# Three of eight token blocks by rows instead of two, with a shorter candidate list and dense sums held in PSUM

## The chip, the cores and the metric

The kernel runs on one core of a Trainium2 chip. The metric is the device time of one execution in microseconds. An execution is one launch from the inputs in HBM to the output in HBM.

## What is computed

A decoder layer: projections, retention and sliding-window attention, a first norm that gives h, and then the PEER feed-forward layer with which this case deals. For each of 1024 tokens and 8 heads, it finds the best 16 of 16384 experts by product keys and sums their outputs:

```
s1, i1 = lax.top_k(s[:, :, 0], K)          # K = 16 of 128 keys, two sides
s2, i2 = lax.top_k(s[:, :, 1], K)
cand = (s1[..., :, None] + s2[..., None, :]).reshape(T, H, K * K)
top_s, pos = lax.top_k(cand, K)            # 16 of 256 pairs
idx = take_along_axis(cand_idx, pos)       # 128 experts per token
g = softmax(top_s)
u = take(u_tab, ib); a = gelu(einsum('cd,ced->ce', xb, u)) * gb
y = einsum('ce,ced->cd', a, take(v_tab, ib))
```

All is float32; u_tab and v_tab have 16384 rows of 1024. The result is layer_norm(ALPHA * h + y).

## The kernel before

The program has five stages, each written engine by engine with its own order and semaphores. `project`, `attend` and `score` (queries, key scores, and the search for token blocks 0 and 1) come first. The last two stages hold the change.

The 1024 tokens are 8 blocks of 128. A block is worked in one of two ways. **Dense** blocks (6 of them) are multiplied with all 16384 experts on TensorE; a one-hot product makes a gate for every pair of token and expert, zero where the expert was not picked. **By rows** (the first GB = UB = 2 blocks), each token's 128 picked rows are gathered: one indirect DMA of GpSimd brings one row of 1024 for each of 128 tokens (0.5 MB), and VectorE makes a dot product or a weighted addition of it. Numbers of float32 go through TensorE in two parts, hi and lo, with three products each.

`experts_in` (z = U h) has 128 tiles of 128 experts in 8 turns of 16 tiles; a tile has two slots, 32 to a turn. Per tile TensorE does 24 products of 512 columns into z_first and 24 of 256 into z_rest, ACT and GpSimd split the tile (L795, L799), ACT reads z and sends it to HBM. Beside this, at slots fixed by tables:
- VectorE's `top_piece` searches one later block per turn in turns 0 to 5: 16 `side` searches in 128 scores, 8 `pairs` searches in 256 sums (L741, then L728 to L732), and 4 `names` (L756 to L764), which turn places into expert numbers for two heads.
- Gate steps, 32 per dense block, in turns FIRST = 2 to 7: one-hot on VectorE (L1273), scaling on ACT, product on TensorE, copy on ACT.
- Row products: GpSimd's gathers (L1215), VectorE's dot products (L1285), PER_TURN of them per turn, in RING = 3 buffers, EARLY = 2 ahead. `gather` waits until the product that used its buffer is done. GpSimd's tile splits stand in the same queue.

`experts_out` (y = V a) has 32 rounds of 4 tiles. Each round, for each dense block: ACT takes the gelu of z, VectorE multiplies by the gate (`product`, L1560), ACT and VectorE split into a_hi and a_lo (L1470, L1564), and TensorE does 2 x 12 products of 512 columns (L1443 to L1445) into two of eight PSUM banks used in turn; VectorE adds both to y in SBUF (`add`, L1572). V's tiles are split by ACT and VectorE (L1475, L1577). Rows of v (GpSimd L1508, VectorE `add_row` L1555) are spread over rounds 1 to 30, in four buffers, three ahead. In round r VectorE works through the blocks in steps: product(r), add(r - 1), split of v, lo of the block before, rows. y starts as ALPHA * h, loaded whole (L1591 scales it).

The buffers of `experts_out` that are filled ahead lie in one piece of memory, `room`, which earlier stages use for their own tiles; the trace calls all of them `room`.

## Time and profile before

| | us |
|---|---|
| three runs | 3078.61, 3078.38, 3083.45 (median 3078.61) |
| the profiled execution | 3082.5, its span 3080.7 |
| granted TensorE clock, mean | 0.985 |
| busy: TensorE 97%, VectorE 76%, ACT 39%, GpSimd 34% | 2980.4, 2327.8, 1204.8, 1053.0 |
| `experts_in` | 741.8 to 2005.8 |
| `experts_out` | 2005.8 to 3080.7 |
| moved by DMA | 693 MB, mean 225 GB/s |

The span is cut at the first product of a turn or of a round. A busy share is an average over stages with different limits, so the stretches are read one by one. Products on TensorE overlap, so their durations add up to more than the span; the price of one is the distance between starts.

### The profile page before, as it was taken

Reading aid. Unit: us, or ns where it says so; the run is one execution under the profiler, and the core shown is the slowest. Engines: PE = TensorE matmul, PEld = TensorE weight load, DVE = VectorE, ACT = ScalarE, POOL = GpSimd, SP = SyncE. Lnnn points to the kernel's source line nnn. Section 1 sums busy time; section 2 is a strip of 40 time slices with the busy share of each in tenths; the row PEclk is TensorE's granted clock in tenths of the full one; section 3 lists DMA queues with packets and bytes.
Section 4 is the critical chain, followed back from the end, with each engine's and each line's share of the span. In section 5 each row is a group of like instructions: output and inputs, shape, how many; then the busy total and the mean of one; then the engine's idle time right before and its main releaser. Section 6 shows DMA issues by size and latency. Waiting matters only on the chain. (4 is left out here: it accounts for less than half of the span.)

```text
span 3080.7 us, 42384 instructions
## 1 busy us (share of the span) xinstructions
PE 2980.4 (97%) x15866; PEld 2565.9 (83%) x15866; DVE 2327.8 (76%) x4289; ACT 1204.8 (39%) x2245; POOL 1053.0 (34%) x750
## 2 busy tenths in 40 slices
PE   7997998999999999999999999979999999999998
PEld 6887886888888899989898999868888888888887
DVE  4214775567988888888887556569998998999898
ACT  2112332222222566656566657533333333333331
POOL 3222221001455443443434454424433333333331
PEclk9997998999999999999999999989999999999999
DMA  4223222222677666666666888789988898888881
GB/s 169 84 89 123 104 97 83 72 79 69 236 247 255 228 225 234 223 246 241 240 231 250 288 299 301 290 297 317 321 299 302 283 313 292 295 307 296 298 306 74
DMA packets 291846, 693.46 MB, mean 225 GB/s; under 512 B 20304, under 2 KB 134352, under 8 KB 288464
## 3 DMA queue, kind: packets, MB, share of 16 engines
q1 hardware_dynamic: 189776, 315.61, 30.7%
q0 software_dynamic: 73728, 268.47, 24.4%
q10 hardware_dynamic: 28160, 106.96, 9.0%
q8 instruction: 113, 1.85, 0.2%
q14 instruction: 69, 0.57, 0.1%
HBM read 564.08 MB, written 126.88 MB: 224 GB/s over the span
## 5 line engine op out<-in xcount | busy, mean ns | idle before, releaser
L1443 PE MATMUL y_ps<-v_hi,a_hi 128*128 128x512 f32 x1536 | 600.1, 391 | 20.4 <-DVE y L1572 11.5
L1444 PE MATMUL y_ps<-v_lo,a_hi 128*128 128x512 f32 x1536 | 599.6, 390 | 0.0
L1445 PE MATMUL y_ps<-v_hi,a_lo 128*128 128x512 f32 x1536 | 599.4, 390 | 0.0
L799 POOL TENSOR_TENSOR u_lo<-u_raw,u_hi 128x1024 fp32r<-128x1024 f32 x128 | 314.6, 2458 | 725.0 <-ACT u_hi L795 724.0
L1104 PE MATMUL z_first<-hT_hi,u_hi 128*128 128x512 f32 x1024 | 409.9, 400 | 9.5 <-PEq L825 5.1
L1508 POOL DMA_INDIRECT v_rows<-in_v,room x192 | 259.7, 1353 | 463.1 <-DVE y L1555 439.2
L1106 PE MATMUL z_first<-hT_hi,u_lo 128*128 128x512 f32 x1024 | 401.3, 392 | 0.0
L1105 PE MATMUL z_first<-hT_lo,u_hi 128*128 128x512 f32 x1024 | 400.7, 391 | 0.0
L1443 PEld LDWEIGHTS y_ps<-v_hi,a_hi 128*128 128x128 f32 x1536 | 289.6, 189 | 81.6 <-issue 11.9
L1445 PEld LDWEIGHTS y_ps<-v_hi,a_lo 128*128 128x128 f32 x1536 | 289.6, 189 | 60.4
L1444 PEld LDWEIGHTS y_ps<-v_lo,a_hi 128*128 128x128 f32 x1536 | 289.6, 189 | 60.3
L1273 DVE TENSOR_TENSOR hot<-near,iT 128x1024 f32<-128x1024 f32 x192 | 234.1, 1222 | 124.2 <-PE g_ps L1114 122.2
L1572 DVE TENSOR_TENSOR y<-y_ps,y 128x512 f32<-128x512 f32 x384 | 255.2, 685 | 80.9 <-PE y_ps L1445 77.6
L1104 PE MATMUL z_rest<-hT_hi,u_hi 128*128 128x256 f32 x1024 | 297.0, 290 | 0.0
L1105 PE MATMUL z_rest<-hT_lo,u_hi 128*128 128x256 f32 x1024 | 289.7, 283 | 0.0
L1106 PE MATMUL z_rest<-hT_hi,u_lo 128*128 128x256 f32 x1024 | 289.6, 283 | 0.0
L1146 ACT ACTIVATE hot_g<-hot,gT 128x128 f32<-128x128 f32 x768 | 244.4, 390 | 77.7 <-DVE hot L1273 50.0
L1285 DVE CUSTOM_DVE_ANT_0 u_rows<-u_rows,h_ps 128x1024 f32<-128x1024 f32 x170 | 207.3, 1219 | 73.7 <-DMA u_rows<-in_u,room 62.0
L1555 DVE SCALAR_TENSOR_TENSOR y<-v_rows,a_rows,y 128x1024 f32<-128x1024 f32 x192 | 242.5, 1278 | 1.7 <-DMA v_rows<-in_v,room 1.7
L1475 ACT ACTIVATE v_hi<-room 128x1024 fp32r<-128x1024 f32 x128 | 135.4, 1058 | 271.7 <-DMA room<-in_v 267.9
L1104 PEld LDWEIGHTS z_first<-hT_hi,u_hi 128*128 128x128 f32 x1024 | 193.7, 189 | 46.4 <-issue 5.2
L1106 PEld LDWEIGHTS z_first<-hT_hi,u_lo 128*128 128x128 f32 x1024 | 193.3, 189 | 42.5
(195 smaller groups left out, 5829.4 us busy)
## 6 DMA issues: line engine op xcount, KB each, us to landing
u_raw<-in_uT SPq DMA_DIRECT2D x128, 512.0 KB
room<-in_v SPq DMA_DIRECT2D x128, 512.0 KB
z<-z_sb ACTq DMA_DIRECT2D x128, 384.0 KB
gates<-g_sb ACTq DMA_DIRECT2D x24, 2048.0 KB
room<-z SPq DMA_DIRECT2D x16, 1536.0 KB
z_in<-z SPq DMA_DIRECT2D x16, 1536.0 KB
g_in<-gates SPq DMA_DIRECT2D x16, 1536.0 KB
room<-gates SPq DMA_DIRECT2D x15, 1536.0 KB
```

The lines of the kernel that those rows point to most:

```text
L799: self.nc.gpsimd.tensor_tensor(self.u_lo[e][:], self.u_raw[e][:], self.u_hi[e][:].bitcast(F32), ALU.subtract).then_inc(self.u_lo_in[e], 1)
L1104: nc.tensor.matmul(o, u_hi[e][:, k], hT_hi[:, k, cols], start=(k == 0), stop=False)
L1105: nc.tensor.matmul(o, u_hi[e][:, k], hT_lo[:, k, cols], start=False, stop=False)
L1106: last = nc.tensor.matmul(o, u_lo[e][:, k], hT_hi[:, k, cols], start=False, stop=(k == KT - 1))
L1146: last = nc.scalar.activation(hot1_g[g][:, t], hot[g][:, 0, t], ACT.Copy, scale=gT[:, t0 + t:t0 + t + 1])
L1273: nc.vector.tensor_tensor(hot[g][:], bc(bc(iota_ps, 1, 4), 1, 2), bc(iT[:, :, t0:t0 + 4], 3, NK), ALU.is_equal).then_inc(hot_in[g], 1)
L1443: nc.tensor.matmul(o, ah, v_hi[p][:, i, c], start=(i == 0), stop=False)
L1444: nc.tensor.matmul(o, ah, v_lo[p][:, i, c], start=False, stop=False)
L1445: last = nc.tensor.matmul(o, al, v_hi[p][:, i, c], start=False, stop=(i == GROUP - 1))
L1508: nc.gpsimd.indirect_dma_start(out=rows_in[i % RING][:], out_offset=None, in_=d["v"].rearrange("a b c -> (a b) c"), in_offset=bass.Indirec ...
L1555: nc.vector.scalar_tensor_tensor(y[:, b], rows_in[i % RING][:], a_rows[:, b, slot:slot + 1], y[:, b], ALU.mult, ALU.add).then_inc(added[b], 1)
L1572: nc.vector.tensor_tensor(y[:, GB + s, c], y_ps[n % 8][:], y[:, GB + s, c], ALU.add).then_inc(y_read, 1)
```

## The change

Three blocks go by rows instead of two, five are dense. In `experts_in` the second half of a tile keeps 256 columns and the first shrinks to 384; there are six row buffers, three of them in `room` (two lie where the first tiles of v will be), and a new table of row products by turn, which ends in the middle of turn 7. Gate steps begin in turn 3. `pairs` searches 80 candidates instead of 256: a pair (a, b) of sorted lists can only be among the best 16 if (a + 1)(b + 1) is at most 16, and four rectangles hold all of these. `decode` turns a place among the 80 into a row and a column, for four heads at once, and `names` then runs twice in a row.

In `experts_out` two of the five dense blocks (HELD) stay in two PSUM banks each for all rounds and are added to y once, at the end. The other three share four banks; they are taken in alternating direction, so that the last of one round is the first of the next and goes on in its banks: two blocks are added per round. The load of h is cut into four, in another order, and ALPHA is applied in a block's first addition. RING and EARLY of this stage stay 4 and 3.

```diff
@@ constants
-GB = 2
+GB = 3
-UB = 2
+UB = 3
@@ class TopK
+    KEPT = [(0, 2, 16), (2, 2, 8), (4, 4, 4), (8, 8, 2)]
...
-        link(nc.vector.tensor_tensor(self.cand[:], bc(self.top[:, 0], 2, TOPK), bc(self.top[:, 1], 1, TOPK), ALU.add))
-        self.top16(link, self.cand[:].rearrange("p a b -> p (a b)"), self.cand_left[:],
-                   self.best[:, b % 2, h], self.pos[:, b % 2, h])
+        at = 0
+        for first, n, wide in self.KEPT:
+            part = self.cand[:, at:at + n * wide].rearrange("p (a c) -> p a c", c=wide)
+            last = nc.vector.tensor_tensor(part, bc(self.top[:, 0, first:first + n], 2, wide),
+                                           bc(self.top[:, 1, 0:wide], 1, n), ALU.add)
+            at += n * wide
+        link(last)
+        self.top16(link, self.cand[:], self.cand_left[:], self.best[:, b % 2, h], self.pos[:, b % 2, h])
...
+    def decode(self, link, b, half):
+
+        nc = self.nc
+        pos = self.pos[:, b % 2, half * PH // 2:(half + 1) * PH // 2]
+        row, col = self.ab[:, 0], self.ab[:, 1]
+        link(nc.vector.tensor_scalar(self.step, pos, 4, None, ALU.logical_shift_right))
+        link(nc.vector.tensor_scalar(self.step, self.step, 1, None, ALU.max))
+        nc.vector.tensor_scalar(self.past, self.step, 16, -16, ALU.mult, ALU.add)
+        link(nc.vector.tensor_scalar(self.step, self.step, -1, 5, ALU.mult, ALU.add))
+        link(nc.vector.tensor_tensor(col, pos, self.past, ALU.subtract))
+        link(nc.vector.tensor_tensor(row, col, self.step, ALU.logical_shift_right))
+        link(nc.vector.tensor_tensor(self.past, row, self.step, ALU.logical_shift_left))
+        link(nc.vector.tensor_tensor(col, col, self.past, ALU.subtract))
...
-        nc.vector.tensor_scalar(self.ab[:, 0], pos, 4, None, ALU.logical_shift_right)
-        link(nc.vector.tensor_scalar(self.ab[:, 1], pos, 15, None, ALU.bitwise_and))
@@ score
-                    if h % 2:
-                        tk.names(link, b, h // 2)
+                    if h % 4 == 3:
+                        tk.decode(link, b, h // 4)
+                        for two in range(2):
+                            tk.names(link, b, h // 4 * 2 + two)
@@ experts_in
-    RING, EARLY = 3, 2
+    RING, EARLY = 6, 5
-    PER_TURN = [24, 34, 27, 27, 27, 27, 45, 45]
+    PER_TURN = [50, 62, 62, 40, 40, 40, 60, 30]
...
+        rows_in = ahead.rows + ahead.v_raw
+        rows_in = rows_in + [sb(f"u_rows{i}", [P, D]) for i in range(RING - len(rows_in))]
...
+            first, end = 6 if s == 0 else 0, SLOTS // 2 if s == TB - 1 else SLOTS
...
+                        sp.wait_ge(h_taken, UB)
...
+                        sp.wait_ge(row_used, UB * PH * TOPK)
                         for e in range(2):
                             sp.dma_start(ahead.v_raw[e][:], d["v"][e]).then_inc(ahead.v_here[e], 16)
...
-                    elif n == 6:
-                        tk.names(link, b, q)
-                    elif n == 7 and q == Q - 1:
-                        v.wait_ge(exps, b + 1)
-                        tk.gates(link, b)
+                    elif n == 6 and q % 2:
+                        tk.decode(link, b, q // 2)
+                        tk.names(link, b, q - 1)
+                    elif n == 7 and q % 2:
+                        tk.names(link, b, q)
+                        if q == Q - 1:
+                            v.wait_ge(exps, b + 1)
+                            tk.gates(link, b)
@@ experts_out
+        HELD = (0, DB - 1)
+        CYCLED = list(range(1, DB - 1))
+        LAST = len(CYCLED) - 1
+
+        def order(r):
+
+            if r == 0:
+                return [HELD[0], *CYCLED[:2], HELD[1], *CYCLED[2:]]
+            return [HELD[0], *(CYCLED[::-1] if r % 2 else CYCLED), HELD[1]]
+
+        def run(r, s):
+
+            return LAST * r + (LAST - CYCLED.index(s) if r % 2 else CYCLED.index(s))
+
+        def banks(r, s):
+
+            first = 2 * HELD.index(s) if s in HELD else 4 + 2 * (run(r, s) % 2)
+            return y_ps[first:first + 2]
+
+        def opens(r, s):
+
+            return r == 0 or (s not in HELD and run(r, s) > LAST * r)
+
+        def closes(r, s):
+
+            return r == NG - 1 or (s not in HELD and run(r, s) < LAST * (r + 1))
+
+        def made(r):
+
+            return order(max(r - 1, 0))
...
                 load_v(0, first=2)
+                load_h(slice(GB + 1, TB - 1), cycled_here)
                 load_z(1)
-                sp.dma_start(y[:], d["h"].rearrange("n p c -> p n c")).then_inc(h_here, 16)
+                load_h(slice(0, GB), rows_here)
                 load_v(1)
+                load_h(slice(GB, GB + 1), held_here)
+                load_h(slice(TB - 1, TB), held_here)
...
-                        nc.tensor.matmul(o, ah, v_hi[p][:, i, c], start=(i == 0), stop=False)
+                        nc.tensor.matmul(o, ah, v_hi[p][:, i, c], start=(opens(r, s) and i == 0), stop=False)
...
-                            wait(pe, y_read, BANKS * r + 2 * s + a - 7)
+                            if s not in HELD and opens(r, s):
+                                wait(pe, y_read, 2 * run(r, s) + a - 3)
...
+                        if first:
+                            ins = nc.vector.scalar_tensor_tensor(part, part, ALPHA, o, ALU.mult, ALU.add)
+                        else:
+                            ins = nc.vector.tensor_tensor(part, o, part, ALU.add)
...
-                        add(r - 1, s)
+                        if closes(r - 1, s):
+                            add(r - 1, s)
```

Three places in the order of instructions. GpSimd in turn 1 of `experts_in`; u_lo is a tile's split, the DMAs are row gathers. Before:

```order
L799 TENSOR_TENSOR u_lo<-u_raw,u_hi 128x1024
L1215 DMA room<-in_u,room 128x1024
L1215 DMA u_rows<-in_u,room 128x1024
L799 TENSOR_TENSOR u_lo<-u_raw,u_hi 128x1024
L1215 DMA u_rows<-in_u,room 128x1024
L1215 DMA room<-in_u,room 128x1024
L799 TENSOR_TENSOR u_lo<-u_raw,u_hi 128x1024
L1215 DMA u_rows<-in_u,room 128x1024 x2
L799 TENSOR_TENSOR u_lo<-u_raw,u_hi 128x1024
L1215 DMA room<-in_u,room 128x1024
```

Now:

```order
L822 TENSOR_TENSOR u_lo<-u_raw,u_hi 128x1024
L1244 DMA u_rows<-in_u,room 128x1024 x3
L1244 DMA room<-in_u,room 128x1024
L822 TENSOR_TENSOR u_lo<-u_raw,u_hi 128x1024
L1244 DMA room<-in_u,room 128x1024 x2
L1244 DMA u_rows<-in_u,room 128x1024
L822 TENSOR_TENSOR u_lo<-u_raw,u_hi 128x1024
L1244 DMA u_rows<-in_u,room 128x1024 x2
L1244 DMA room<-in_u,room 128x1024 x2
L822 TENSOR_TENSOR u_lo<-u_raw,u_hi 128x1024
```

Between two splits stand three to four gathers where there were two.

VectorE in the same stage, a pairs search and the names behind it; ISA with h_ps is a dot product. Before:

```order
L741 TENSOR_TENSOR room<-top 128x256
L728 MAX best<-room 128x8
L729 MAX_INDEX pos<-best,room 128x8
L730 MATCH_REPLACE room<-best,room 128x256
L731 MAX best<-room 128x8
L732 MAX_INDEX pos<-best,room 128x8
L1285 ISA u_rows,room<-u_rows,h_ps 128x1024
L1285 ISA room 128x1
L756 TENSOR_SCALAR ab<-pos 128x32
L757 TENSOR_SCALAR ab<-pos 128x32
L758 TENSOR_TENSOR room<-ab,places 128x1024
L762 TENSOR_TENSOR room<-room,top_i 128x512 x2
```

Now, from within a search of the candidates to the first five of eight decode operations:

```order
L734 MATCH_REPLACE room<-best,room 128x80
L735 MAX best<-room 128x8
L736 MAX_INDEX pos<-best,room 128x8
L1317 ISA u_rows,room<-u_rows,h_ps 128x1024
L1317 ISA room 128x1
L1317 ISA u_rows,room<-u_rows,h_ps 128x1024
L1317 ISA room 128x1
L764 TENSOR_SCALAR step<-pos 128x64
L765 TENSOR_SCALAR step<-step 128x64
L766 TENSOR_SCALAR past<-step 128x64
L767 TENSOR_SCALAR step<-step 128x64
L768 TENSOR_TENSOR ab<-pos,past 128x64
```

The searched list has 80 elements for 256, and eight decode operations for four heads stand where two stood for two.

VectorE in `experts_out`, the first steps of a round. Before:

```order
L1560 TENSOR_TENSOR z_in<-z_in,g_in 128x4x128
L1572 TENSOR_TENSOR y<-y_ps,y 128x512 x2
L1577 TENSOR_TENSOR v_lo<-room,v_hi 128x1024
L1555 SCALAR_TENSOR_TENSOR y<-v_rows,a_rows,y 128x1024
L1560 TENSOR_TENSOR z_in<-z_in,g_in 128x4x128
L1572 TENSOR_TENSOR y<-y_ps,y 128x512 x2
L1577 TENSOR_TENSOR v_lo<-room,v_hi 128x1024
L1564 TENSOR_TENSOR a_lo<-z_in,a_hi 128x4x128
L1555 SCALAR_TENSOR_TENSOR y<-v_rows,a_rows,y 128x1024
L1560 TENSOR_TENSOR z_in<-z_in,g_in 128x4x128
L1572 TENSOR_TENSOR y<-y_ps,y 128x512 x2
```

Now:

```order
L1637 TENSOR_TENSOR z_in<-z_in,g_in 128x4x128
L1658 TENSOR_TENSOR y<-y_ps,y 128x512 x2
L1663 TENSOR_TENSOR v_lo<-room,v_hi 128x1024
L1641 TENSOR_TENSOR a_lo<-z_in,a_hi 128x4x128
L1632 SCALAR_TENSOR_TENSOR y<-v_rows,a_rows,y 128x1024
L1632 SCALAR_TENSOR_TENSOR y<-room,a_rows,y 128x1024
L1637 TENSOR_TENSOR z_in<-z_in,g_in 128x4x128
L1663 TENSOR_TENSOR v_lo<-room,v_hi 128x1024
L1641 TENSOR_TENSOR a_lo<-z_in,a_hi 128x4x128
L1632 SCALAR_TENSOR_TENSOR y<-v_rows,a_rows,y 128x1024 x3
```

The pair of additions out of y_ps is missing from the third step, and two or three row additions stand in a step that had one or two.

## Rows read from the trace of the kernel before

**Rows 1.** The profile by stretches: eight turns of experts_in, then parts of experts_out; columns head first.

```profile
core 0: us, PE busy (x) PEld busy (x) DVE busy (x) ACT busy (x) POOL busy (x), PEclk, DMA share, GB/s
741.80:882.70 140.90, 138.09 (x768) 121.38 (x769) 125.39 (x350) 32.47 (x50) 64.06 (x42) 0.97 0.61 214
882.70:1016.20 133.50, 133.50 (x771) 118.17 (x770) 113.25 (x295) 32.90 (x49) 70.99 (x50) 1.00 0.71 249
1016.20:1179.10 162.90, 162.90 (x1029) 146.98 (x1028) 138.82 (x314) 100.21 (x209) 66.91 (x44) 1.00 0.64 228
...
1342.20:1505.10 162.90, 162.90 (x1029) 147.00 (x1028) 139.87 (x318) 101.36 (x210) 66.19 (x43) 1.00 0.66 236
...
1668.20:1831.20 163.00, 163.00 (x1030) 147.07 (x1028) 94.85 (x131) 101.33 (x209) 81.39 (x62) 1.00 0.79 284
1831.20:2005.80 174.60, 164.76 (x1030) 147.81 (x1028) 98.51 (x135) 108.81 (x221) 79.19 (x62) 0.99 0.82 298
2005.80:2054.00 48.20, 36.69 (x145) 29.70 (x146) 25.19 (x28) 12.53 (x20) 4.80 (x5) 0.84 0.83 296
2054.00:2090.40 36.40, 34.59 (x146) 28.11 (x145) 33.34 (x43) 12.53 (x20) 17.79 (x10) 0.95 0.96 333
2090.40:3037.00 946.60, 946.60 (x4178) 783.82 (x4177) 861.77 (x1073) 314.07 (x465) 326.64 (x242) 1.00 0.86 294
```

**Rows 2.** TensorE in order of time, a 256-column product of experts_in; start, length, line.

```profile
1307.28 0.28 PE L1104 MATMUL z_rest<-hT_hi,u_hi 128*128 128x256 f32 x1
...
1307.64 0.28 PE L1104 MATMUL z_rest<-hT_hi,u_hi 128*128 128x256 f32 x1
```

**Rows 3.** Groups of instructions by line and shape, 742 to 2006 us.

```profile
L799 POOL TENSOR_TENSOR u_lo<-u_raw,u_hi 128x1024 fp32r<-128x1024 f32 x127 | 312.3, 2459 | 509.7 <-ACT u_hi L795 508.8 <-issue 0.7
...
L1273 DVE TENSOR_TENSOR hot<-near,iT 128x1024 f32<-128x1024 f32 x192 | 234.1, 1222 | 124.2 <-PE g_ps L1114 122.2 <-issue 1.4
...
L758 DVE TENSOR_TENSOR room<-ab,places 128x1024 f32<-128x1024 uint32 x26 | 32.0, 1230 | 0.9
...
L762 DVE TENSOR_TENSOR room<-room,top_i 128x512 f32<-128x512 f32 x52 | 63.1, 1254 | 0.9
...
L731 DVE MAX8 top<-room 128x8 f32<-128x128 f32 x100 | 29.5, 295 | 3.4
...
L731 DVE MAX8 best<-room 128x8 f32<-128x256 f32 x50 | 21.4, 428 | 1.7
...
L732 DVE FIND_INDEX8 pos<-best,room 128x8 uint32<-128x256 f32 x50 | 20.9, 419 | 0.0
...
L756 DVE TENSOR_SCALAR ab<-pos 128x32 uint32<-128x32 uint32 x26 | 13.8, 532 | 0.1
...
L757 DVE TENSOR_SCALAR ab<-pos 128x32 uint32<-128x32 uint32 x26 | 4.5, 173 | 0.0
```

**Rows 4.** GpSimd and VectorE in order of time: a row gather and the dot product that waited.

```profile
1829.21 0.94 POOL L1215 DMA_INDIRECT u_rows<-in_u,room  x1 [2.39 <-DVE room L1285]
...
1833.79 1.22 DVE L1285 CUSTOM_DVE_ANT_0 u_rows<-u_rows,h_ps 128x1024 f32<-128x1024 f32 x1 [1.81 <-DMA u_rows<-in_u,room]
```

**Rows 5.** The chain that ended last, in order of time, start of experts_out.

```profile
2008.36 27.21 DMA y<-h
```

**Rows 6.** Groups of instructions by line and shape, VectorE, one round of experts_out.

```profile
L1572 DVE TENSOR_TENSOR y<-y_ps,y 128x512 f32<-128x512 f32 x12 | 8.1, 686 | 3.2 <-PE y_ps L1445 3.1
L1555 DVE SCALAR_TENSOR_TENSOR y<-v_rows,a_rows,y 128x1024 f32<-128x1024 f32 x6 | 7.7, 1279 | 0.0
```

**Rows 7.** The profile by stretches of 10 and 30 us.

```profile
1910.00:1920.00 10.00, 10.00 (x68) 9.18 (x67) 5.10 (x7) 6.63 (x16) 5.20 (x4) 1.00 0.99 408
...
2160.00:2190.00 30.00, 30.00 (x134) 24.85 (x133) 28.81 (x37) 10.97 (x17) 11.80 (x9) 1.00 0.96 324
```

**Rows 8.** GpSimd and VectorE in order of time: a gather in experts_out and its addition.

```profile
2083.66 2.63 POOL L1508 DMA_INDIRECT v_rows<-in_v,room  x1 [0.30 <-issue]
...
2095.49 1.28 DVE L1555 SCALAR_TENSOR_TENSOR y<-v_rows,a_rows,y 128x1024 f32<-128x1024 f32 x1 [0.49 <-DMA v_rows<-in_v,room]
```

More of the change, by code:

```diff
@@ L1025, in own_rows @@
         def own_rows(s, k):
[L1027 to L1029 removed]
+            first, end = 6 if s == 0 else 0, SLOTS // 2 if s == TB - 1 else SLOTS
+            n = end - first
+            at = [sum(PER_TURN[:s]) + PER_TURN[s] * min(max(j - first, 0), n) // n for j in (k, k + 1)]
+            return range(at[0], at[1])
         def steps_at(s, k):
@@ L1302, in _ @@
                 for b in range(2):
-                    tk.names(link, b, PH // 2 - 1)
+                    tk.decode(link, b, 1)
+                    for two in range(Q // 2, Q):
+                        tk.names(link, b, two)
                     v.wait_ge(exps, b + 1)
```

139 lines of the change are left out of this document (78 added, 61 removed).

## The prediction

> **What bounds the kernel now.** The times first. The three runs have a median of 3078.6 us; the profiled execution took 3082.5 us with a span of 3080.7. All sums below stand against that execution, and 3.9 us come off at the end. What a measurement of this kernel can tell from no change is about 0.2%, 6 us.
>
> Then the profile by stretches, cut where the kernel's loops begin anew [rows 1]. The eight turns of `experts_in` (16 tiles of experts each) take 134 to 175 us, and TensorE is busy for all of each but for the first and last. `experts_out` is 32 rounds: the first two take 48.2 and 36.4 us, and rounds 2 to 30 take 946.6 us, 32.64 each, TensorE busy throughout at the full granted clock. So TensorE sets the pace of both stages. But the same rows show who is next. VectorE is busy 140 us of a 163 us turn and 861.8 of 946.6 us (29.7 of a round's 32.64), and the DMA engines' share is 0.79 to 0.86 there, 0.96 in round 1. The change moves an eighth of the tokens from TensorE to the two that stand just behind it. That is the question of this case.
>
> **TensorE.** In `experts_out` 4178 products of 512 columns take 946.6 us [rows 1], 0.2266 us each. In `experts_in` three 256-column products take 0.36 us, 0.12 each [rows 2]. A 384-column product lies between; by the line through both it takes 0.173, so each of the 384 first-half products of a turn saves 0.053: 20.5 us per turn. Turn 2 also loses its 32 steps of gate products, which is what it has over turn 1: 162.9 - 133.5 = 29.4 us. TensorE alone would then need 120, 113, 113, 142.6 (three times), 142.5 and 154.1 us for the eight turns. A round of `experts_out` has 120 products for 144: 27.2 us. Were TensorE still the bound everywhere, the change would bring 193 us in `experts_in` and 174 in `experts_out`. I expect neither.
>
> **experts_in, turns 0 to 5: VectorE becomes the bound.** The 128 dot products of the third block all lie here (turns 0 to 5 had 166, now 294), at 1.2 us each [rows 4].
> - Pairs: MAX8 takes 0.428 us for 256 elements and 0.295 for 128, so 0.245 for 80. The index operation goes by the same slope, 0.236 from 0.419, and the replacement like it [rows 3]. Two, two and one of them save 0.92 us per head, 7.3 a turn. The one addition becomes four small ones; at the 0.173 of L757 each [rows 3] they take at most 0.7 us where 0.4 to 0.8 stood: nothing.
> - Decode: eight small linked operations per four heads, some 0.2 us each, against four of 0.53 and 0.17 [rows 3]: about +0.5, +1 per turn.
> - Turn 0 begins with the names of four heads per block, where it had two: two more sets of 1.23 and 2 x 1.25 us [rows 3], with a reduction counted like the first, are +10.
> - Turn 2 loses 32 one-hot operations of 1.22 us [rows 3], -39.
>
> VectorE's busy time by turn is then, from the stretches [rows 1]:
> turn 0: 125.4 + 26 x 1.2 - 9.2 + 10 + 2 = 159 us;
> turn 1: 113.3 + 28 x 1.2 - 7.3 + 1 = 141;
> turn 2: 138.8 + 35 x 1.2 - 7.3 - 39 + 1 = 135;
> turns 3 to 5: 140.0 + 13 x 1.2 - 7.3 + 1 = 149 each.
> All six stand above TensorE's numbers, and their sum is 883 us where these turns now take 926.
>
> TensorE can't run ahead of this: GpSimd's split of the next tile stands behind gathers that wait for a dot product, with six buffers as with three. Turn 1 shows it in the order: up to four gathers between two splits where there were two. A bound engine still loses some time to waits. Its floor is none; its ceiling is the 9% that VectorE idles in rounds 2 to 30, 80 us. I take 25, since its queue now always has work behind the waits. Turns 0 to 5: 908 us, **-18** (range -43 to +37).
>
> One row speaks against even this. The first shift of the old decode (L756) has a mean of 0.532 us and the second, of the same shape, 0.173 [rows 3]: the first one was held up. The Trainium skill (SBUF — State Buffer, Who interferes with whom) says that a VectorE operation with two SBUF inputs, or one in a two-port mode, locks GpSimd out or is locked out for a whole instruction. By that rule each of the twelve new decodes could wait out a GpSimd split of 2.46 us [rows 3], 30 us in all; by the measured mean, which the terms above hold, it is 0.36 us each.
>
> **experts_in, turns 6 and 7.** VectorE has time there (95 + 15 x 1.2 us of 143). The DMA engines have less. Turn 6 moves 284 GB/s x 163 us = 46.3 MB; 15 more gathers of 0.524 MB come and 1 MB of z goes: 53 MB. At 284/0.79 = 359 GB/s that is 148 us, at the 408 of a short stretch [rows 7] 130. I take 145, a gain of 18; turn 7 has fewer gathers than before and gains TensorE's 20: **-38**. The sync queue has a new wait in turn 7, for all 384 dot products, ahead of the first two loads of v, because three row buffers lie where v will. Behind it queue the expert tiles 124 to 127, which TensorE needs. All dot products are due in the turn's first half and the wait comes behind it, so I count nothing; were VectorE late, TensorE would wait as long.
>
> The searches of heads 0 to 3 and 4 to 7 in the stage before are now followed by names for four heads at once, which can delay one weight split of VectorE: **+2** (0 to +8). The sum to here is -54.
>
> **experts_out.** Rounds 0 and 1: the chain holds a 27.2 us load of y from h [rows 5], after which VectorE scaled all of y. Now the first additions need three blocks of h, loaded ahead of z, and the scaling is folded into them. Two rounds of 27.2 at full clock are the floor (-30); with loads at 333 GB/s [rows 1] still ahead of round 1, I take 68 us for 84.6: **-16**. The last round loses 24 products: **-5**. The tail after it keeps its form, one block's additions and norm.
>
> Rounds 2 to 30, one round each:
> - TensorE: 27.2 us.
> - VectorE: 4 additions for 12, 10 products and splits of z for 12 (the same shape and price, 0.686), 12.8 row additions for 8.53 at 1.279 [rows 6]: 29.7 - 10 x 0.686 + 4.27 x 1.279 = 28.3 us.
> - DMA: 12.8 gathers are 6.7 MB, v 2.1, z and gates 1.3 each: 11.4 MB for the 9.6 of 294 GB/s x 32.64 us. Round 1 moved 333 GB/s at a share of 0.96 [rows 1], 347 when full: 32.9 us. The 324 at 0.96 of another stretch give 34; the 408 at 0.99 [rows 7], in `experts_in` without the gates' 512-byte pieces, give 28.
>
> So DMA is the bound if it keeps its rate of this stage. I take 32.0, nearer to its own stage's price than to the other's, because the added bytes are all 4 KB rows. 29 x (32.0 - 32.64) = **-19**; the range of 28.3 to 35 is -126 to +68. A rule gives nearly the same: the Trainium skill (DMA: Bandwidth & Descriptors, Specifications) has 358 GB/s as a core's share of HBM, which would make 31.9 us; its fabric ceiling of 435 would make 26.3. The 408 GB/s above is over the first, so the trace doesn't bear it out as a hard limit.
>
> Holding two blocks in PSUM leaves four banks for the other three, where TensorE was eight banks ahead of VectorE. Its price is nothing while VectorE reads within a block's time (5.4 us); a longer stall now reaches TensorE at once, which is in the upper end.
>
> **Sum.** -18 - 38 + 2 - 16 - 5 - 19 = -94; 3082.5 - 94 - 3.9 = **2985 us**.
>
> **Rivals.**
> 1. *DMA keeps up* (0.24). Short stretches at 400 GB/s speak for it. Rounds run at VectorE's 28.3 and some wait, 29: 29 x 3.6 = -105 for -19. 2985 - 86 = 2899 us.
> 2. *The gathers' round trip becomes the wait* (0.09), the case that ends slower. `experts_out` keeps four row buffers. A buffer is free again only after issue, landing and addition. From a gather's issue to its use by a waiting engine were 4.6 us in a calm stretch [rows 4], but 11.8 in a full one [rows 8]; plus 1.3 for the addition that is 13.1 us for four rows, 42 us for 12.8. Against it: VectorE waited for a row there only briefly (0.49 us). All terms outside rounds 2 to 30 are -75, so it decides from 32.64 + 75/29 = 35.2 us a round, a trip of 11 us. At 36 us: 3078.6 - 75 + 97 = 3101 us.
> 3. *experts_in gains nothing* (0.12): the heavy slots (decode and names of four heads back to back, some 9 us where a slot is 4.5) stall TensorE, which one-hot and gate steps tie to within a slot of VectorE. Turns 0 to 5 come out at +37: 2985 + 55 = 3040 us.
>
> **Chances and range.** The forecast has 0.55; together 1. Faster by over 0.2%: the forecast and rivals 1 and 3, less a share for a bad DMA stage on top of them: 0.87. Same 0.04, slower 0.09. The range reaches down to rival 1 and up past rival 3: 2890 to 3060.
>
> **What would show it.** In turns 0 to 5 VectorE's busy share above 0.95 and turns of 150 us; turn 1 longer than the 133.5 of before. In turn 6 a share of DMA above 0.9. In `experts_out` a share above 0.95 at some 355 GB/s, rounds of 32 us, TensorE with short waits each round for additions or a_lo, VectorE waiting for v_rows. No `y<-h` of 27 us in the chain. If rounds take 29 us, the DMA price is wrong; if VectorE waits for rows while the share is below 0.9, it is the four buffers.

## The result, and the profile after

The changed kernel takes 3141.3 us (median of 4 runs, 3137.9 to 3142.1) against 3080.4 us for the kernel before on the same chip: ratio 1.0191, 95% interval 1.0179 to 1.0203. It is slower by 61 us, where 94 us less were forecast and the range ended at 3060. The profiled execution took 3137.9 us with a span of 3135.8, 55 more than the profiled execution of before.

The same view as [rows 1], of the changed kernel: turns 0, 1, 4, 6 and 7 of `experts_in`, then rounds 0, 1 and 2 to 30 of `experts_out` and the rest.

```profile
core 0: us, PE busy (x) PEld busy (x) DVE busy (x) ACT busy (x) POOL busy (x), PEclk, DMA share, GB/s
739.80:903.50 163.70, 126.52 (x769) 124.94 (x769) 152.84 (x437) 31.98 (x52) 88.12 (x67) 0.86 0.74 259
903.50:1063.80 160.30, 123.58 (x769) 120.60 (x770) 148.20 (x387) 30.09 (x49) 98.06 (x79) 0.90 0.86 296
...
1383.60:1540.50 156.90, 146.19 (x1029) 145.21 (x1029) 146.74 (x375) 99.80 (x210) 76.72 (x56) 0.97 0.80 282
...
1698.20:1847.80 149.60, 144.06 (x1030) 143.37 (x1029) 118.08 (x167) 99.57 (x209) 95.97 (x77) 0.98 0.93 352
1847.80:1998.40 150.60, 143.89 (x1030) 142.42 (x1028) 81.39 (x106) 105.31 (x220) 63.16 (x45) 0.99 0.73 279
1998.40:2036.20 37.80, 30.71 (x121) 24.82 (x122) 16.84 (x21) 12.35 (x18) 2.45 (x3) 0.87 0.89 318
2036.20:2086.60 50.40, 30.78 (x122) 24.56 (x121) 39.70 (x42) 10.55 (x16) 24.71 (x19) 0.83 0.95 338
2086.60:3090.00 1003.40, 862.10 (x3482) 684.50 (x3481) 827.74 (x892) 284.70 (x405) 529.09 (x362) 0.94 0.93 325
3090.00:3135.80 45.80, 27.85 (x121) 22.07 (x119) 38.18 (x57) 1.26 (x2) 10.61 (x7) 0.91 0.20 80
```

Against [rows 1] the 55 us split like this:

| part | before | after | moved | forecast |
|---|---|---|---|---|
| start of `experts_in` | 741.8 | 739.8 | -2 | +2 |
| turns 0 to 5 | 926.4 | 958.4 | +32 | -18 |
| turns 6 and 7 | 337.6 | 300.2 | -37 | -38 |
| rounds 0 and 1 | 84.6 | 88.2 | +4 | -16 |
| rounds 2 to 30 | 946.6 | 1003.4 | +57 | -19 |
| last round and tail | 43.7 | 45.8 | +2 | -5 |

TensorE is no longer busy throughout anywhere. Turn 1, which took 133.5 us on TensorE before, takes 160.3 with VectorE busy 148.2. A round takes 34.6 us for 32.64, and VectorE, TensorE and the DMA engines all have room in it: busy 28.5 us, busy 29.7 us, share 0.93. No engine is full, so a wait sets the pace. The waits of the changed kernel between 2120 and 2980 us name it (engine and line, what ended the wait, total us, times, longest):

```profile
POOL v_rows L1585 <- DVE y L1632: 267.1, 156, 4.5
...
DVE y L1632 <- DMA v_rows<-in_v,room: 118.0, 90, 3.6
POOL room L1585 <- DVE y L1632: 94.8, 59, 3.7
PEld y_ps L1516 <- DVE a_lo L1641: 73.8, 24, 5.0
PE y_ps L1516 <- DVE a_lo L1641: 63.4, 23, 4.6
...
DVE y L1632 <- DMA room<-in_v,room: 31.8, 30, 3.4
```

GpSimd waits for an addition to free a buffer, VectorE waits for a row to land, and TensorE waits for VectorE's a_lo, which stands in the queue behind that addition. In order of time, a gather of GpSimd (start, length of its issue) and the addition of VectorE that waited for it:

```profile
2460.27 2.63 POOL L1585 DMA_INDIRECT v_rows<-in_v,room  x1 [0.30 <-issue]
...
2470.60 1.29 DVE L1632 SCALAR_TENSOR_TENSOR y<-v_rows,a_rows,y 128x1024 f32<-128x1024 f32 x1 [0.86 <-DMA v_rows<-in_v,room]
```

From issue to use by a waiting VectorE are 10.3 us, 11.6 with the addition: 2.9 us a row with four buffers. Over all gathers issued between 2200 and 2950 us, the trace's DMA records give a mean of 6.98 us from issue to the last byte (90% under 9.2), 1.99 to the start of the addition and 1.95 until the buffer's next gather (the addition itself lies in this part): 10.9 us a cycle, 2.73 us a row, and a round has 12.8 rows, 34.9 us.

That sum alone proves nothing: a ring of four buffers always has a cycle of four times its pace, whoever sets the pace. What tells is how the cycle is filled. In the kernel before, the same records give 6.60 us to the last byte, then 6.89 in which the landed row lies waiting for VectorE, then 1.82: 15.3 us. Nearly half of that cycle was slack; now 1.99 us of it are left on average, and VectorE waits at 120 of the 317 additions of the rows above. The mean trip without slack (6.98 + 1.95 = 8.9 us) would by itself allow 28.6 us a round, so by this sum it is the uneven part that costs: rows that land late, and two or three additions in a row, with no buffer to even them out. How the two share in it was not separated. The chain that ended last passes through the same wait in the same window; before, TensorE was 32% of the chain over the span, now it is 0%:

```profile
2447.22 0.69 DVE z_in L1637
2447.91 0.73 DVE v_lo L1663
...
2460.27 10.30 DMA v_rows<-in_v,room
2470.60 1.30 DVE y L1632
2472.15 7.96 DMA v_rows<-in_v,room
```

In turns 0 to 5 VectorE hardly waits for anyone. Groups of VectorE by line and shape, 739.8 to 1698.2 us (busy us, mean ns, idle before and what ended it):

```profile
L1317 DVE CUSTOM_DVE_ANT_0 room<-room,h_ps 128x1024 f32<-128x1024 f32 x147 | 179.5, 1221 | 15.2 <-DVE top_i L736 2.0 <-DMA room<-in_u,room 1.9 <-issue 1.0
L1317 DVE CUSTOM_DVE_ANT_0 u_rows<-u_rows,h_ps 128x1024 f32<-128x1024 f32 x144 | 175.8, 1221 | 15.3 <-DVE top_i L736 3.5 <-issue 0.9 <-DMA u_rows<-in_u,room 0.9
L1305 DVE TENSOR_TENSOR hot<-near,iT 128x1024 f32<-128x1024 f32 x96 | 117.0, 1221 | 10.0 <-PE g_ps L1143 9.7
L748 DVE TENSOR_TENSOR room<-top 128x32 f32<-128x32 f32 x50 | 38.5, 771 | 0.2
...
L1317 DVE DVE_READ_ACCUMULATOR2_ANT room<- 128x1 f32 x291 | 24.0, 83 | 0.0
L748 DVE TENSOR_TENSOR room<-top 128x16 f32<-128x16 f32 x150 | 22.1, 201 | 0.0
L764 DVE TENSOR_SCALAR step<-pos 128x64 uint32<-128x64 uint32 x14 | 16.1, 1150 | 0.0
```

Of its 65 idle us (958.4 less the 893.3 busy of six turns), 9.7 end with a gate product and 2.8 with a row. Most of the rest, 51.5 us, are gaps of under 0.25 us, 27 of them before the 291 dot products (30.5 us stand before them in all) and the others mostly between the small operations of the searches. TensorE's waits of the same stretch end on the tile split of GpSimd, which stands behind gathers, which stand behind dot products:

```profile
PE z_first L1133 <- POOL u_lo L822: 128.9, 31, 17.5
```

### The profile page after: what moved, and what is told of

It reads as the page before. It is cut to its first block and busy times, and to the rows that moved or that the text cites. A ratio compares the mean times of both kernels' runs of the same rounds, so it can differ in the third digit from the quotient of the medians.

```text
span 3135.8 us, 40748 instructions
## 1 busy us (share of the span) xinstructions
PE 2728.5 (87%) x14839; PEld 2417.3 (77%) x14839; DVE 2379.6 (76%) x4584; ACT 1089.0 (35%) x2021; POOL 1375.7 (44%) x1006
## 3 DMA queue, kind: packets, MB, share of 16 engines
q1 hardware_dynamic: 173584, 299.35, 28.3%
## 5 line engine op out<-in xcount | busy, mean ns | idle before, releaser
L1585 POOL DMA_INDIRECT v_rows<-in_v,room x288 | 415.4, 1442 | 352.5 <-DVE y L1632 312.5
L1517 PE MATMUL y_ps<-v_lo,a_hi 128*128 128x512 f32 x1280 | 521.3, 407 | 0.0
L1518 PE MATMUL y_ps<-v_hi,a_lo 128*128 128x512 f32 x1280 | 519.1, 406 | 0.0
L1133 PE MATMUL z_first<-hT_hi,u_hi 128*128 128x384 f32 x1024 | 370.4, 362 | 140.2 <-POOL u_lo L822 134.8
L1632 DVE SCALAR_TENSOR_TENSOR y<-v_rows,a_rows,y 128x1024 f32<-128x1024 f32 x288 | 364.2, 1281 | 140.0 <-DMA v_rows<-in_v,room 139.8
L1134 PE MATMUL z_first<-hT_lo,u_hi 128*128 128x384 f32 x1024 | 358.1, 350 | 0.0
L1135 PE MATMUL z_first<-hT_hi,u_lo 128*128 128x384 f32 x1024 | 357.5, 349 | 0.0
L1244 POOL DMA_INDIRECT u_rows<-in_u,room x192 | 184.7, 962 | 174.6 <-DVE room L1317 142.9
L1244 POOL DMA_INDIRECT room<-in_u,room x192 | 184.2, 959 | 171.9 <-DVE room L1317 135.0
L1317 DVE CUSTOM_DVE_ANT_0 room<-room,h_ps 128x1024 f32<-128x1024 f32 x192 | 234.2, 1220 | 26.7 <-DMA room<-in_u,room 8.8
```

The source lines that it names most:

```text
L1133: nc.tensor.matmul(o, u_hi[e][:, k], hT_hi[:, k, cols], start=(k == 0), stop=False)
L1134: nc.tensor.matmul(o, u_hi[e][:, k], hT_lo[:, k, cols], start=False, stop=False)
L1135: last = nc.tensor.matmul(o, u_lo[e][:, k], hT_hi[:, k, cols], start=False, stop=(k == KT - 1))
L1244: nc.gpsimd.indirect_dma_start(out=rows_in[r][:], out_offset=None, in_=d["u"], in_offset=bass.IndirectOffsetOnAxis(ap=ahead.picked[:, b, s ...
L1317: nc.vector.tensor_tensor_reduce(rows_in[r][:], rows_in[r][:], h_ps[:], 1.0, 0.0, ALU.mult, ALU.add, ahead.z_rows[:, b, slot:slot + 1]).th ...
L1517: nc.tensor.matmul(o, ah, v_lo[p][:, i, c], start=False, stop=False)
```

## The experiments

The theory after reading this had two halves: (A) rounds go by the gathers' round trip through four buffers, and (B) turns 0 to 5 go by the sum of VectorE's work. Rivals to A were the bytes and VectorE itself; to B the bursts, decode and names of four heads in two neighbouring slots.

### experts_out: buffers, bytes, or VectorE

**e1, six row buffers in `experts_out`**

```diff
-    RING, EARLY = 4, 3
+    RING, EARLY = 6, 5
```

> The changed kernel with six instead of four row buffers (five gathers ahead instead of three) in experts_out; nothing else. Theory 1, the round trip: four rows take one trip of 10.9 us (7.0 us from issue to landing), 2.73 us a row, and that sets the 34.6 us of a round. Then six buffers take away most of the 165 us that VectorE waits for rows in rounds 2 to 30, rounds fall to 30 to 32 us and the time to 3010 to 3060 us. Theory 2, bandwidth: the DMA engines are full at a share of 0.93 and 325 GB/s. Then a round stays at 34 to 35 us, the landing takes as much longer as there are more gathers in flight (about 10 us), and the time stays at 3130 to 3150 us.

3070.3 us, ratio 0.9956 (0.9939 to 0.9972): 71 us less than the change, and a little faster than the kernel before. Rounds 2 to 30 take 939.9 us. Theory A holds against its rival: two more buffers give back more than the 61 us lost. But both of its numbers were set too low (30 to 32 us a round, 3010 to 3060 us), so with six buffers something else holds the rounds, which e6 and e9 look for.

**e3, only the first four gathers of `experts_out`.** The other 380 rows aren't fetched; every addition is kept and reads one of the four.

```diff
-                        if k + EARLY < ROWS:
+                        if k + EARLY < RING:
...
-                    v.wait_ge(row_here[i % RING], 16 * (i // RING + 1))
+                    v.wait_ge(row_here[i % RING], 16)
```

> The changed kernel without the gathers of experts_out but for the first four; VectorE adds the same four rows again and again, 384 additions as before, and doesn't wait for them. So the output leaves out most of the v rows of the three blocks. Both theories on rows say that rounds fall to VectorE's own 28.3 to 29.5 us; the time to 2960 to 2990 us. If rounds stay above 31 us, neither rows nor DMA hold them, but the tie between TensorE and VectorE (four banks, a_lo one or two blocks ahead) or the tiles of v that arrive late.

2941.7 us, ratio 0.9541 (0.9525 to 0.9557). Rounds 2 to 30 take 28.2 us each with VectorE busy for all of it: the forecast's 28.3 for VectorE was right, and the gathers cost the change 200 us.

**e6, half rows; e9, half rows and six buffers.** In both, a gather fetches 2 KB per token (a half row, from another place of v) where it fetched 4, and each addition reads the half twice. In the trace such a gather is 64 packets of 4 KB where it was 128, so bytes and packets are halved together, and these runs can't tell them apart. e9 has RING, EARLY = 6, 5 besides.

```diff
-                        out=rows_in[i % RING][:], out_offset=None, in_=d["v"].rearrange("a b c -> (a b) c"),
+                        out=rows_in[i % RING][:, 0:D // 2], out_offset=None,
+                        in_=d["v"].rearrange("a b (h c) -> (a b h) c", h=2),
...
```

> The changed kernel with four row buffers in experts_out, whose gathers there fetch 2 KB (the first or second half of a row) where they fetched 4 KB, as many of them and as many additions of 1024 elements (each reads the half twice): half of the gathered bytes are left out. Theory 'the trip is long because the 16 engines are full': the gather falls from 7.0 us towards the 4.6 us of a calm place, a cycle of a buffer from 10.9 to some 8.5 us, 2.1 us a row, under VectorE's 28.2 us a round: 2945 to 2965 us, near the run without gathers (2942). Rival 'the trip is fixed by issue and descriptors (128 of them), whatever their size': it stays near 7 us, the rounds at 34 us, 3110 to 3140 us.

> Run e6 (half of each row gathered, 3035 us, 31.1 us a round) with six row buffers in place of four: neither the engines' bytes nor the round trip should bind. Theory: with four buffers and whole rows two things stand over VectorE's 28.2 us a round, the trip (34.6 against 32.4 us with six) and the bytes (32.4 against what this run shows). Then the rounds 2 to 30 fall to 28.3 to 29 us each, in all 2945 to 2965 us, by the run without gathers (2942 us). Rival 'descriptors or GpSimd's issue bind, not bytes': they stay at 31 to 32 us, 3030 to 3060 us.

e6 took 3034.9 us (0.9857, 0.9841 to 0.9874), between both its expectations; e9 2958.2 us (0.9595, 0.9581 to 0.9609), as its theory said. Rounds 2 to 30 of e1, e6, e9 and e3, in this order (columns as in [rows 1]):

```profile
2089.70:3029.60 939.90, 829.24 (x3482) 662.66 (x3481) 823.14 (x895) 283.78 (x405) 610.59 (x362) 0.97 0.96 347
```

```profile
2087.60:2988.80 901.20, 824.38 (x3481) 663.40 (x3480) 823.61 (x896) 276.93 (x405) 536.31 (x363) 0.98 0.79 255
```

```profile
2082.20:2913.90 831.70, 798.25 (x3482) 650.76 (x3481) 819.87 (x895) 280.06 (x405) 639.23 (x362) 1.00 0.84 276
```

```profile
2081.90:2899.00 817.10, 796.26 (x3481) 651.14 (x3481) 815.92 (x896) 279.04 (x405) 2.99 (x2) 1.00 0.51 165
```

| us per round | whole rows | half rows | no rows |
|---|---|---|---|
| four buffers | 34.6 | 31.1 | 28.2 |
| six buffers | 32.4 | 28.7 | |

Read down, the columns price the two buffers at 2.2 to 2.4 us a round; read across, the bytes are worth 3.5 to 3.7. Each of these has a scatter that the table hides. Rounds 2 to 30 of whole rows and six buffers, unchanged, took 921.4, 922.9, 935.4, 939.9 and 955.9 us in the profiled executions of e11, e8, e12, e1 and e10, 31.8 to 33.0 us a round; with four buffers they took 1003.4, 999.1 and 1003.7 in the change, e4 and e7. So with whole rows the buffers are worth 1.5 to 2.8 us, and with six buffers the bytes 3.1 to 4.3. Within this, each acts alike whatever the other is. With half rows and four buffers the engines' share is 0.79 and the rounds are still 2.9 us over VectorE's 28.2, and two more buffers take away 2.4 of them: there it is mostly the trip. With whole rows and six buffers the share is 0.96 at 347 GB/s, and VectorE still waits 66 us for rows between 2120 and 2980 us, where it was 150: there it is mostly the bytes (VectorE now also waits 23 us for ScalarE's part of the tiles of v and 21 for its part of z and gates, whose loads are late; in the change neither shows). The trip from issue to the last byte is 6.98 us with whole rows and 5.01 with half, with four buffers; with six it is 7.91 and 5.51, with more transfers in flight on the same engines.

### experts_in: VectorE's sum, or the bursts

**e2, two blocks with all else of the change; e5, the same with names by two.** e5 decodes two heads and names them in the slot n = 6 of every quarter turn; e2 keeps the four-head bursts.

```diff
-GB = 3
+GB = 2
-UB = 3
+UB = 2
-    PER_TURN = [50, 62, 62, 40, 40, 40, 60, 30]
+    PER_TURN = [24, 34, 34, 33, 33, 33, 40, 25]
```

e5 has these edits and, in `top_piece`, with `decode` cut to two heads:

```diff
-                    elif n == 6 and q % 2:
-                        tk.decode(link, b, q // 2)
-                        tk.names(link, b, q - 1)
-                    elif n == 7 and q % 2:
-                        tk.names(link, b, q)
+                    elif n == 6:
+                        tk.decode(link, b, q)
+                        tk.names(link, b, q)
...
```

> Everything of the change but the third block: GB = UB = 2, with 80 candidates, six buffers in experts_in, sums held in PSUM (two of six blocks), the new order of the h loads; the row products are spread 24, 34, 34, 33, 33, 33, 40, 25 over the turns. If the third block's rows alone made the kernel slower, this one is at or below the kernel before: turns of 163 us, rounds of 32.6, rounds 0 and 1 together 10 to 16 us shorter, 3060 to 3080 us. The rival, that the narrower coupling of the held sums (four banks for the blocks that are added) or the names in pairs cost time by themselves, gives rounds above 33.2 us or turns above 165, and 3090 us or more.

> The two-block kernel with the change's other parts (run e2: 3123 us), with decode and names again for two heads at a time, in the slot n = 6 of every quarter turn, where the kernel before had names. In e2 the turns 3 to 7 take 170 us where the kernel before has 163, with TensorE waiting for VectorE once per half turn and its clock at 1.2 GHz for some 7 us after it. Theory 'burst': it is decode and names of four heads in two neighbouring slots that holds up make_hot, then the gate matmuls, then TensorE. Then the turns come back to 163 to 165 us: five turns by 6 and turn 0 by some 3, in all 3080 to 3095 us. Rival 'row buffers and traffic': the loads of 34 rows a turn or the six buffers do it; then it stays at 3115 to 3130 us.

e2 took 3122.7 us (1.0134, 1.0117 to 1.0151), on its rival's side: with two blocks the rest of the change alone costs 40 us, against the kernel before on the same chip. e5 (3087.0 us; 1.0024, 1.0014 to 1.0034) is 7 us over the kernel before on its own chip, so it gives 34 of the 40 back. Turn 4 of e2, then of e5:

```profile
1360.30:1531.20 170.90, 165.53 (x1030) 148.73 (x1028) 139.96 (x362) 101.07 (x210) 69.74 (x49) 0.98 0.68 243
```

```profile
1342.40:1505.80 163.40, 163.30 (x1030) 147.17 (x1029) 145.29 (x378) 101.37 (x210) 70.33 (x49) 1.00 0.70 255
```

In e5 VectorE does 5 us more in a turn that is 7.5 us shorter. TensorE is the bound here, and a stall of it is not caught up: it waits for the late split or gate, and after each of three waits of 4.1 us it runs for 3 to 7 us at the 1.2 GHz level (mean granted clock 0.98 for the turn, 1.00 in e5). TensorE's waits for GpSimd's split in turns 3 to 5 of e2, which e5 doesn't have:

```profile
PE z_first L1133 <- POOL u_lo L822: 12.2, 3, 4.1
```

The rounds of both take 32.64 us each as before, so the held sums and the four shared banks, which tie TensorE closer to VectorE, cost nothing as long as VectorE is on time.

**e4, names by two with three blocks**, the second part of e5's diff alone.

> The changed kernel with the decode for two heads at a time and the names where they stood before: one set in slot 6 of every eight instead of two in every sixteen; this is eight more small decode operations of 0.2 us twice a turn, about 3.5 us. Theory of the heavy slots: turns 0 to 5, now 958 us, fall by 15 to 35 us since TensorE no longer stalls for 8 us at a time and keeps its clock; 3105 to 3125 us. Rival: VectorE's sum alone sets these turns; then they get 10 to 20 us longer, 3150 to 3160 us.

3158.5 us (1.0252, 1.0234 to 1.0270), 17 us more than the change. **e7, all 256 pairs and the old names** (TopK as before; h_own in memory of its own) goes the same way:

> The changed kernel with the search among all 256 sums and the decoding of the kernel before (two operations of VectorE per two heads), h_own outside the shared room for it. By the rows of the two traces a turn then has 7.2 us more of searches on VectorE, 3 us or so less of additions where GpSimd doesn't hold them up and up to 8 us less where it does, 3 to 4 us less of decoding. Theory 'VectorE's sum bounds turns 0 to 5': each moves by the net of these, -4 to +4 us, in all 3120 to 3165 us. Rival 'the burst of decode and names costs here too': the turns fall by 6 us each and more, under 3110 us.

3154.5 us (1.0237, 1.0220 to 1.0254). Turn 1 of e4, then of e7, where the change has 160.3 us and 148.2 busy:

```profile
903.90:1069.50 165.60, 129.44 (x770) 127.00 (x769) 154.51 (x401) 31.45 (x50) 95.95 (x79) 0.88 0.84 286
```

```profile
903.30:1070.60 167.30, 130.21 (x769) 127.74 (x769) 157.31 (x355) 31.13 (x50) 96.41 (x79) 0.90 0.85 283
```

Both take VectorE's work out of bursts and give it more of it: 6 and 9 us more busy time, 5 and 7 us more turn. So with three blocks theory B holds, and the rival falls as the main cause. It is not nothing: VectorE's idle time in turns 0 to 5 falls from 65 us to 55 in e4 and 49 in e7, but its busy time grows by 33 and 41. The two kernels answer to the same edit with opposite signs: spreading the names is worth 34 us where TensorE is the bound and costs 17 where VectorE is.

Most of e4's 33 us is not the work of eight more small operations. It is that more of them are held up by GpSimd. In order of time, a tile split of GpSimd in the changed kernel, and the first shift of a decode, which takes 0.18 us elsewhere:

```profile
982.54 2.42 POOL L822 TENSOR_TENSOR u_lo<-u_raw,u_hi 128x1024 fp32r<-128x1024 f32 x1
...
982.61 2.40 DVE L764 TENSOR_SCALAR step<-pos 128x64 uint32<-128x64 uint32 x1
```

Count in turns 0 to 5 every operation of VectorE that is over 0.15 us longer than its form is in a calm place (the shortest tenth). There are 30 in the kernel before, which lose 56 us together, 31 with 60 us in the change, and 45 with 83 us in e4. All but one in each of the last two lie over a tile split, and each of those ends as long after the split's end as its own calm length, within 0.15 us: it waits the split out.

### Versions that might beat both

**e8, e1 with 30 rows moved from turns 0 to 5 to turn 7** (from slot 11 there the rows use the four buffers that are not v_raw); **e12, 20 rows moved and v_raw loaded 8 slots later.** The diff is e8's; e12 has the table 48, 59, 59, 36, 36, 36, 60, 50 and slot 19 for 11.

```diff
-    PER_TURN = [50, 62, 62, 40, 40, 40, 60, 30]
+    PER_TURN = [46, 57, 57, 35, 35, 35, 60, 59]
...
+        CYCLE = own_rows(TB - 1, 11).start
+        OURS = [r for r in range(RING) if r not in range(1, 3)]
+        held = [i % RING if i < CYCLE else OURS[i % len(OURS)] for i in range(UB * PH * TOPK)]
...
```

> Run e1 (six row buffers in experts_out, 3070 us) with 30 rows moved from the first six turns of experts_in to the last (46, 57, 57, 35, 35, 35, 60, 59 a turn): from slot 11 of the last turn the rows go round the four buffers that are not v_raw, which can then be loaded as before. Theory 'VectorE bounds turns 0 to 5, TensorE turns 6 and 7': 30 dots of 1.37 us leave the first, 41 us, and lie beside TensorE in the last, whose VectorE is busy 82 of 150 us: turns 0 to 5 at 151 us each, in all 3025 to 3040 us. Rival 'turn 7's transfers': its four buffers and the loads of z, gates and v there make the dots late, and first_product with them; then turn 7 and round 0 grow by 15 us or more and 3050 to 3070 us is left.

> Run e8 (3058 us, six row buffers in experts_out and 59 rows in the last turn of experts_in) with the slots of the change as they are, 50 rows in the last turn (48, 59, 59, 36, 36, 36, 60, 50) and v_raw loaded 8 slots later, so that all six buffers serve until slot 19 of that turn. Theory: what e8 lost in turn 7 (28 us) is mostly its ring of four and full engines; with fewer rows and six buffers turn 7 takes 160 to 165 us, turns 0 to 5 some 934 us, in all 3040 to 3055 us. Rival 'turn 7 is bound by its transfers for any row more': each row moved there costs what it saves in turns 0 to 5, and 3055 to 3070 us comes out.

e8: 3058.1 us (0.9934, 0.9917 to 0.9950), the fastest that computes the whole. Turns 0 to 5 fell by 37 us against e1, where 30 dot products 1.37 us apart are 41; but turn 7 grew by 28 (the row below; 150.1 us and 0.73 in e1), with VectorE waiting 45 us for rows. Its rival was right about the place. Of the 12 us between the medians of e1 and e8, 9 can come from there. The profiled executions are 29.5 us apart, and 17 of these lie in rounds 2 to 30, where the code is the same.

```profile
1814.70:1992.70 178.00, 149.75 (x1029) 146.50 (x1028) 115.45 (x164) 104.78 (x220) 90.35 (x74) 0.94 0.85 321
```

e12: 3060.9 us (0.9943, 0.9931 to 0.9956). Turn 7 took 159.7 us and turns 0 to 5 took 943.3, where its theory had 934: less moved, less won on both sides, and the two intervals overlap.

**e11, e1 with evened slots** (names of heads 2 and 3 in the third quarter, rows of a turn placed where the search leaves room); **e10, that with 17 rows moved to turn 7.**

```diff
+        WEIGHT = [18, 18, 6, 18, 18, 6, 26, 26,
+                  18, 18, 6, 18, 18, 6, 6, 0,
+                  18, 18, 6, 18, 18, 6, 0, 26,
+                  18, 18, 6, 18, 18, 6, 0, 0]
...
+            w = [WEIGHT[j] if s < TB - 2 else 1 for j in range(first, end)]
```

> Run e1 (six row buffers in experts_out, 3070 us; rows per turn as in the change) with the evened slots of e10 alone. Theory 'VectorE's sum bounds turns 0 to 5': its 147 to 153 us a turn stay, and only the idle time of 7 to 12 us a turn can shrink: 3035 to 3060 us. Rival: nothing moves, 3065 to 3075 us.

> Run e8 (3058 us) with two changes in experts_in: 47 rows in the last turn in place of 59 (48, 59, 59, 37, 37, 37, 60, 47), and VectorE's load evened within a turn: names of heads 2 and 3 go to the third quarter, away from decode, and the rows of turns 0 to 5 stand in the slots by the room that the search leaves (none or one beside decode and names, two or three in the free slots). Theory: in e8 turn 7 lost 28 us to full engines (393 to 414 GB/s in its first 60 us) and its ring of four, and turns 0 to 5 still had 10 to 16 us each in which VectorE stood idle beside TensorE's stalls behind the bursts. Turn 7 falls to 155 to 165 us, turns 0 to 5 to 148 to 152 us each: 3020 to 3040 us. Rival 'VectorE's idle time there is loads of rows, not bursts': the turns stay at 154 to 156 us, and 3045 to 3060 us is left.

Both came out slower than both sides of their expectations: 3085.6 us (1.0010, 0.9998 to 1.0022) and 3089.6 us (1.0017, 1.0003 to 1.0032). Turn 4 of e11 has 154.24 us of VectorE where the change has 146.74, with the same instructions, in a turn of 162.2 us. Over turns 0 to 5 it is 918.7 us for 893.4, 25 more, and the turns are 978.7 us for the 961.2 of e1. The trace says what lengthened them: 48 operations lie over a tile split and lose 81 us, where it was 31 and 60. One group, 0.18 us each in a calm place, over turns 0 to 5 of e11 (771 ns on average in the change):

```profile
L748 DVE TENSOR_TENSOR room<-top 128x32 f32<-128x32 f32 x50 | 50.0, 999 | 0.2
```

The profiled execution of e11 took 3070.8 us, the least of its ten, because its rounds 2 to 30 took only 921.4.

e10 loses the gain from its moved rows in the same way, with 48 such operations and 81 us: its VectorE is busy 899.4 us in turns 0 to 5, 6 more than the change although 17 dot products have left. Its runs spread over 29 us (3076 to 3106); the profiled one is the slowest, with 955.9 us in rounds 2 to 30.

## Why the prediction was wrong

- **Rounds 2 to 30** (forecast 32.0 us, measured 34.6; 76 of the 149 us of error). VectorE's 28.3 stands (28.2 in e3) and so does the DMA price: at a share of 0.96 e1 moves 347 GB/s, 361 when full, against the forecast's 347, and its rounds take 32.4. The step that failed is that VectorE's wait for rows was put at nothing: the sum took the slowest engine's pace, and left the round trip of the four buffers to rival 2 with a weight of 0.09, because VectorE had waited only 0.49 us at the gather of [rows 8]. But that row was taken at 8.5 rows a round, one per 3.8 us; four buffers pay for a trip of 15 us at that pace and 10 at the new one. The forecast had both 11.8 us of a full stretch and the limit of 11 us in hand and set them aside. Its own pace, 32.0 us for 12.8 rows, leaves a cycle of 10.0 us for four buffers. The trace of before had 6.60 + 1.82 = 8.4 us of trip and 6.89 of slack in its 15.3, so 1.6 us of slack were to be expected, too little beside trips of which one in ten took 8.5 us or more to land. e1 is what shows it: two buffers more, nothing else, and the rounds take 32.4 us. Rival 2 named 36 us and 3101; its mechanism and place were right, with one reservation: it took the 11.8 us of a single gather for the typical trip, so that its 36 us come near 34.6 in part by luck.
- **Turns 0 to 5** (forecast 908 us, measured 958; 50 us of error). VectorE becomes the bound, as forecast. Its work was 893 us for 883, so the sum was right within 1% (for the terms in it, see the next point): turn 0 has 152.8 for 159, turns 1 and 2 have 148.2 and 146.8 for 141 and 135. The term that was mis-sized is the idle time: 25 us taken, 65 measured. It isn't waiting for others; the forecast priced a dot product at 1.2 us, and back to back they start 1.37 us apart (1.22, then 0.08 for reading the accumulator, then a gap). 291 of them at 0.17 are 49 us, of which the busy times hold 24 and the idle time 25. The 24 are not all new: the busy times that the forecast started from had the accumulators of the 166 old ones in them. Its range (-43 to +37) held the +32.
- Within that, candidate additions were counted as nothing and decodes as +0.36 us of hold-up each. The additions of 50 heads take 60.6 us where the old ones took 38.0, and the 14 decodes 45.4 us where the old shifts took 18.3. Of this, the first addition of a head takes 0.77 us on average, where 34 of the 50 take under 0.2, and the first shift of a decode 1.15 us where 0.18 would do: 43 us held up in these two. In turn 1 the two shifts take 2.40 us, which is the length of a tile split on GpSimd (2.40). The Trainium skill (SBUF — State Buffer, Who interferes with whom) has the rule for this, and the trace agrees: the held operations wait the split out. The forecast had weighed it at 30 us for the shifts against the measured mean of 0.36 and took the mean; the trace stands halfway, at 14 us. But others lost what these gained: the 128x512 products by two took 1254 ns before [rows 3] and 728 after, 27 us less. All hold-ups together went from 56 us to 60, and the sum came out within 1% because terms that were wrong by 20 us and more cancelled, which was luck.
- **Rival 3** had the right size (+37) by the wrong mechanism: bursts. With three blocks e4 shows that spreading them costs. In e2 it is real, at 34 us.
- **Turns 6 and 7**: -37 for -38, of two misses that cancel. Turn 6 is 149.6 us for the 145 taken, at 352 GB/s and a share of 0.93, with the forecast's 53 MB; turn 7 is 150.6 for 154. The new wait of the sync queue costs nothing there.
- **Rounds 0 and 1** (68 forecast, 88.2 measured). The failed step is that the 27.2 us load of h, once out of the chain, was counted as 16 us won. The forecast named the loads still to come at 333 GB/s but did not add up their bytes: both rounds move 29 MB at shares of 0.89 and 0.95, and 68 us would need 428 GB/s. The chain there holds 14.9 us in which the sync queue issues the second load of h, and an 8.6 us load of v that stands behind it, where it had the 27.2 us load of h [rows 5]. The gathers are not the whole of it: e3 with four of them still takes 81.5 us. And with two blocks, in e2 and e5, the new loads gain nothing either: 88.9 and 89.3 us for 84.6.
- **Two claims that held**: the held sums take 108 us off VectorE (753.5 us in rounds 2 to 30 of e5 for 861.8 [rows 1]) and cost nothing there; turn 7, priced with TensorE's product of 384 columns, takes 150.6 us for 154.

## What to carry to other kernels

When a change raises the pace of a ring of buffers, work out first how long a trip the ring can bear at the new pace (buffers times the time per item) and compare it with the trip under the load to come, not with how long the consumer waits today. Read how long landed items lie waiting for their use: here it was 6.89 us of a 15.3 us cycle, and the new pace took 5.3 us off the cycle. A ring needs some of that slack, because trips and uses are uneven. When the bound moves to another engine, price that engine's work by the distance between starts, its gaps included. And test an edit in the kernel where it will live, since spreading VectorE's bursts was worth 34 us with two blocks and cost 17 with three.

## What the runs showed of the hardware

- A gather of 128 rows of 4 KB by GpSimd takes 7.0 us on average from its issue to the last byte with four in flight and the engines at a share of 0.93, 7.9 with six at 0.96, and with rows of 2 KB 5.0 and 5.5. The Trainium skill (DMA: Bandwidth & Descriptors, Anatomy of one DMA — SWDGE (gpsimd) path) gives 2.0 us plus the bytes at 436 GB/s for one transfer, 3.2 us for 0.524 MB by that estimate and 2.6 for half of it. The trace, which is of many transfers at once, is at twice that, and half the bytes (in half the packets) take 2.0 us off instead of 0.6.
- Small operations of VectorE beside a GpSimd tile split last up to the split's own length (2.40 us for an operation of 0.18). In five traces (before, the change, e4, e10, e11) 200 of the 202 operations of turns 0 to 5 that were held up lay over a split, and ended their own calm length after its end, within 0.15 us. With other slots it was 81 us of hold-up in e11 for 60, with the same operations.
- The full engines move 361 GB/s in `experts_out` (e1: 347 at a share of 0.96), close to the 358 of the Trainium skill's rule that the forecast cited (DMA: Bandwidth & Descriptors, Specifications). In `experts_in` the trace is over it: 15 us of turn 7 in e8 held 414.

```profile
1830.00:1845.00 15.00, 13.41 (x96) 12.69 (x95) 12.10 (x17) 9.71 (x23) 8.05 (x7) 1.00 1.03 414
```

- TensorE's granted clock falls to 1.2 GHz after its longer stalls: in turn 1 after those of 10.3 and 9.4 us and two of the three of 3.6 us, for 3 to 14 us each. Its mean is 0.86 to 0.90 in turns 0 to 2, where 28 waits for a tile split make 108 us, the longest 17.5. No run isolates what that costs while VectorE is the bound; in e2, with TensorE as the bound, it is part of the 7.5 us a turn.
